# Chunked scan issued in rounds, with two gate units between its steps

## What is computed

```python
h = rms_norm(x, norm1_pre)
q, k, v, z, xbc, dt_raw, gates = split_cols(h @ w_in, IN_SPLITS)
attn_out = gqa_attention(q, k, v) @ w_attn_proj
# ssd_branch: xbc through a width-5 convolution and silu gives xs, bm, cm;
# for each direction (forward, flipped), 16 heads in 2 groups, 4 chunks of 128 tokens:
y_diag = einsum("bclgn,bcsgn->bcgls", cc, bc) * decay_in, times xd
states = einsum(bc, decay_states, xd)
def step(h, inp): st, dec = inp; return h * dec + st, h      # over the chunks
y_off  = einsum(cc, prev, exp(a_cs))
y = y_fwd + y_bwd + d_skip * xs
ssd_out = rms_norm(y * silu(z), ssd_norm) @ w_ssd_proj
g_attn, g_ssd = split(sigmoid(gates))
mixed = (g_attn * attn_out + g_ssd * ssd_out) @ w_out
```

## Time and profile before

| what | value |
|---|---|
| median of 3 runs | 2350.87 us (2345.10 to 2355.63) |
| the profiled execution | 2345.79 us, span 2344.0 us |
| PE busy | 2198.4 us, 94% of the span |
| DVE, ACT, POOL busy | 49%, 43%, 41% |
| mean granted TensorE clock | 0.961 |

### The profile page before, as it was taken

The page is one execution under the profiler, slowest core; times in us unless marked ns, Lnnn a source line. Parts: engine busy times, 40 slices in busy tenths (PEclk is TensorE's granted clock), DMA queues, the critical chain, the costliest instruction groups (busy, mean ns, idle before and its releaser), DMA issues.

```text
span 2344.0 us, 28202 instructions
## 1 busy us (share of the span) xinstructions
PE 2198.4 (94%) x10837; PEld 1826.0 (78%) x10848; DVE 1142.7 (49%) x1836; ACT 1004.5 (43%) x2027; POOL 962.0 (41%) x730
## 2 busy tenths in 40 slices
PE   7999899999988997899999998998899999999997
PEld 5788778888877776778888877785697887888886
DVE  3445565554344666465554363664445335544322
ACT  5666444443235555244443254655243234323222
POOL 3655553433457652444333442224323334322232
PEclk9999999999999999799999997998899999999998
DMA  4111122232213221122222221110012232222221
GB/s 157 55 55 60 49 99 99 90 108 99 94 60 102 82 68 39 62 82 90 98 100 97 88 88 36 37 36 19 19 46 101 88 108 72 92 106 90 101 99 52
DMA packets 29846, 183.08 MB, mean 78 GB/s; under 512 B 3984, under 2 KB 4112, under 8 KB 11920
## 3 DMA queue, kind: packets, MB, share of 16 engines
q1 hardware_dynamic: 29712, 181.27, 22.4%
HBM read 174.97 MB, written 2.10 MB: 76 GB/s over the span
## 4 chain that ended last, share of the span: by engine, by line
PE 82%; DVE 6%; ACT 5%; issue 3%; POOL 2%; DMA 1%; SPq 0%; POOLq 0%; ACTq 0%; DVEq 0%
PE PS L1452 81%; PE PS L1577 1%; POOL LO L2735 1%; DVE bQS L2191 1%; PE PS L1690 0%; ACT HI L1779 0%; DMA RAW<-wall 0%; DVE aQS L2191 0%; DVE T_f L2263 0%; DVE XL L2268 0%; DVE YH L2293 0%; PE PS L1625 0%; POOL cQ L2818 0%; ACT bP L1995 0%; POOL cROT L2810 0%
## 5 line engine op out<-in xcount | busy, mean ns | idle before, releaser
L2735 POOL TENSOR_TENSOR LO<-RAW,HI 128x512 fp32r<-128x512 f32 (+2 forms) x382 | 540.9, 1432 | 601.6 <-ACT HI L1779 601.3
L1452 PE MATMUL PS<-XH,HI 128*128 128x512 f32 (+1 forms) x1584 | 637.6, 403 | 24.5 <-DVE XL L2191 6.7
L1452 PE MATMUL PS<-XH,LO 128*128 128x512 f32 (+1 forms) x1584 | 624.4, 394 | 0.0
L1452 PE MATMUL PS<-XL,HI 128*128 128x512 f32 (+1 forms) x1584 | 618.1, 395 | 1.0 <-DVE XL L2268 1.0
L1779 ACT ACTIVATE HI<-RAW 128x512 fp32r<-128x512 f32 (+3 forms) x668 | 365.4, 608 | 171.3 <-PE PS L1452 168.0
L2191 DVE TENSOR_TENSOR LO<-RAW,HI 128x512 fp32r<-128x512 f32 (+2 forms) x286 | 305.0, 1071 | 246.2 <-ACT HI L1779 245.8
L1452 PEld LDWEIGHTS PS<-XH,HI 128*128 128x128 f32 (+1 forms) x1584 | 302.2, 191 | 87.7 <-issue 20.4
L1452 PEld LDWEIGHTS PS<-XH,LO 128*128 128x128 f32 (+1 forms) x1584 | 301.4, 190 | 65.7 <-issue 0.8
L1452 PEld LDWEIGHTS PS<-XL,HI 128*128 128x128 f32 (+1 forms) x1584 | 300.8, 190 | 62.7 <-DVE XL L2268 2.5
L1452 PE MATMUL PS<-HH,HI 128*128 128x512 f32 x528 | 205.4, 389 | 0.0
L1452 PE MATMUL PS<-HL,HI 128*128 128x512 f32 x528 | 205.4, 389 | 0.0
(11 more groups left out here) (395 smaller groups left out, 3358.3 us busy)
## 6 DMA issues: line engine op xcount, KB each, us to landing
RAW<-wall SPq DMA_DIRECT2D x138, 1024.0 KB, 4.8
RAW<-wall SPq DMA_DIRECT2D x24, 896.0 KB, 4.4
bROT<-bTQ SPq DMA_DIRECT2D x64, 64.0 KB, 2.0
RAW<-wall SPq DMA_DIRECT2D x5, 512.0 KB, 3.3
XF<-xT SPq DMA_DIRECT2D x4, 512.0 KB, 5.2
outT<-XR SPq DMA_DIRECT2D x8, 256.0 KB, 2.0
FP<-cfp SPq DMA_DIRECT2D x1, 1024.0 KB, 6.7
MKF<-cmask SPq DMA_DIRECT2D x1, 704.0 KB, 10.8
```

The costliest lines, as they stand in the source:

```text
L1452: return e.matmul(out, a, b, start=start, stop=stop)
L2735: return e.tensor_tensor(out, x, h.bitcast(F32), ALU.subtract)
```

## The change

The scan is one generator, `scan()`, that goes in rounds. The elementwise part of each step is a step of its own (`se` for the exponentials, `sz`, `sq`, `sv` for DVE's part of `sy`, `so`, `sp`; `sd` for the decay of the state) and stands one round or more behind the matmuls it reads. All heads use banks 2 and 3, `sp` has banks 4 and 5, `so` bank 6, `sy` bank 7. The states are in an order written out by hand (`STATES`), and a state of chunk 1 has a buffer of its own. Gate units `cga` 0 and `cgs` 0 are moved from behind the z units to the scan, which runs beside them at 1.8 pieces a tick. What is left behind the z units begins with `cpa` 0, then `cga` 1, the transposes, and `cps` 0 at once behind these. The sigmoids of both moved gates are taken right after `yn`.

```diff
-    out += [...] + [("cx", j // 2) for j in CONV[::2]] + [("cz", i) for i in range(4)]
-    for i in range(4):
-        out += [("cga", i), ("cpa", i), ("cgs", i), ("cps", i)]
+    out += [...] + [("cx", j // 2) for j in CONV[::2]] + [("cga", 0), ("cgs", 0)]
+    out += [("cz", i) for i in range(4)] + [("cpa", 0), ("cga", 1), ("cps", 0)]
+    for i in range(1, 4):
+        out += [("cga", i)] * (i > 1) + [("cpa", i), ("cgs", i), ("cps", i)]
...
+            r = 0
+            while sdone[0] < 16 or not finished[0]:
+                while item(r - 3) and ("cxt", CONV[-1]) not in steps:
+                    yield
+                if item(r):
+                    put("sw", *item(r))
+                    if item(r)[1]:
+                        put("sd", *item(r))
+                if r < 16:
+                    for dr in range(2):
+                        at_bank(("sh", r, dr), 2 + dr)
+                    put("sh", r)
+                    yield
+                if item(r - 2):
+                    s = put("sv", *item(r - 2))
+                    freed[ag.bank_of[("sp",) + item(r - 2)]] = ("sprv" if s[2] else "sprv0", s)
+                if item(r - 4):
+                    dr, idx, g = item(r - 4)
+                    freed[6] = ("sod", put("sq", dr, idx + 1, g))
+                    finished[0] = r - 4 == len(STATES) - 1
+                if item(r - 1):
+                    s = ("sp",) + item(r - 1)
+                    at_bank(s, 4 + s[1])
+                    put(*s)
+                    yield
+                if r < 16:
+                    s = put("se", r)
+                    for dr in range(2):
+                        freed[2 + dr] = ("sem", s)
+                if item(r - 3):
+                    dr, idx, g = item(r - 3)
+                    at_bank(put("so", dr, idx + 1, g), 6)
+                    yield
+                if 0 < r < 17:
+                    put("em", r - 1)
+                if 2 < r < 19:
+                    freed[7] = ("syd", put("sz", r - 3))
+                    sdone[0] = r - 2
+                if 1 < r < 18:
+                    at_bank(put("sy", r - 2), 7)
+                    yield
...
-        alongside(scans(), RATES[3])
-        until(lambda: sdone[0] >= 4 and all(finished))
+        alongside(scan(), RATES[3])
+        gate("cga", 0, True)
+        gate("cgs", 0, True)
+        until(lambda: sdone[0] >= 4 and finished[0])
+        beside[1] = RATES[7]
...
-        mix_a(0)
+        for kind in ("mga", "mgs"):
+            for j in range(2):
+                put(kind, 0, j)
+        shares(0)
+        gate("cga", 1)
         for j in range(8):
             b, s = pick(), ("yt", j)
...
-        for i in range(4):
-            if i:
-                mix_a(i)
-            mix_b(i)
+        mix(0)
...
-            elif kind == "sh":
+            elif kind == "se":
                 h, = a
                 if h == 0:
                     e.wait_ge(*when("cdec", "cae"))
                 if h > 1:
                     e.wait_ge(*when("sy", "sy", h - 2))
```

More of the change, by code:

```diff
@@ L347, in unit_sequence @@
     out += [("up1", j) for j in range(FF)] + down("dn1")
-    out += [("cq", 0), ("ck", 0), ("cq", 1), ("cv", 0)] + [("cx", j // 2) for j in CONV[::2]] + [("cz", i) for i in range(4)]
-    for i in range(4):
-        out += [("cga", i), ("cpa", i), ("cgs", i), ("cps", i)]
+    out += [("cq", 0), ("ck", 0), ("cq", 1), ("cv", 0)] + [("cx", j // 2) for j in CONV[::2]] + [("cga", 0), ("cgs", 0)]
+    out += [("cz", i) for i in range(4)] + [("cpa", 0), ("cga", 1), ("cps", 0)]
+    for i in range(1, 4):
+        out += [("cga", i)] * (i > 1) + [("cpa", i), ("cgs", i), ("cps", i)]
     out += [("co", i) for i in range(4)]
@@ L1055, in c_times_b @@
             freed[6] = ("scbd", s)
[L1057 to L1091, removed]
-                    yield
[L1093 to L1110, removed]
-                    for dr in range(2):
[L1112 to L1129, removed]
-                    yield
-            for _ in range(2):
-                for dr in range(2):
-                    next(left[dr])
-                    yield
@@ L1136, in scans, with scan, item, skip_term @@
[L1136 to L1142, removed]
+        def scan():
+            skipped = [0]
+            def item(n):
+                return STATES[n] if 0 <= n < len(STATES) and STATES[n] else None
+            def skip_term(n):
+                for h in range(skipped[0], min(16, skipped[0] + n)):
+                    put("y0", h)
+                    skipped[0] = h + 1
+            r = 0
+            while sdone[0] < 16 or not finished[0]:
+                while item(r - 3) and ("cxt", CONV[-1]) not in steps:
+                    yield
+                if item(r):
[3 more added lines that the diff above has]
+                if r < 16:
+                    for dr in range(2):
+                        at_bank(("sh", r, dr), 2 + dr)
+                    put("sh", r)
+                    yield
+                if item(r - 2):
[9 more added lines that the diff above has]
+                    put(*s)
+                    yield
+                if r < 16:
[14 more added lines that the diff above has]
+                    yield
+                if ("cxt", 7) in steps:
+                    skip_term(4)
+                elif skipped[0] < 10:
+                    skip_term(2)
+                r += 1
@@ L1151, in second, with gate, product @@
             c_times_b(g)
[L1152 to L1157, removed]
-        alongside(scans(), RATES[3])
-        until(lambda: sdone[0] >= 4 and all(finished))
+        def gate(kind, i, later=False):
+            for j, t in enumerate(lin_fm((kind, i), "X", evac=lambda j, t: product(kind, i, j, t))):
+                if not later:
+                    put("m" + kind[1:], i, j)
+        def product(kind, i, j, t):
+            freed[tiles[t].bank] = ("mgr", put("mgp", "m" + kind[1:], i, j, t))
+        alongside(scan(), RATES[3])
[3 more added lines that the diff above has]
+        beside[1] = RATES[7]
         for i in range(4):
@@ L1168, in second, with shares, mix @@
         put("yn")
[L1170 to L1172 removed]
+        def shares(i):
             for j, t in enumerate(lin_fm(("cpa", i), "cO")):
                 freed[tiles[t].bank] = ("mpa", put("mpa", i, j, t))
[L1176 to L1178 removed]
+        def mix(i):
             for j, t in enumerate(lin_fm(("cps", i), "cY")):
@@ L1189, in second @@
             ready["cY", j] = ("yl", s)
-        for i in range(4):
-            if i:
-                mix_a(i)
-            mix_b(i)
+        mix(0)
+        for i in range(1, 4):
+            if i > 1:
+                gate("cga", i)
+            shares(i)
+            gate("cgs", i)
+            mix(i)
         for i in range(4):
@@ L2139, in scalar @@
                 act(dst, src, ACT.Copy, scale=col("dskip", h)).then_inc(SEM["sy0"], 1)
-            elif kind == "sp" and a[1] == 0:
+            elif kind == "sv" and a[1] == 0:
                 dr, idx, g = a
-                e.wait_ge(*when("sst", *step))
-                act(blk(PRV, 2 * dr + g), PS[bank][:, :], ACT.Copy).then_inc(SEM["sprv0"], 1)
-            elif kind == "sh":
+                e.wait_ge(*when("sst", "sp", *a))
+                act(state(*a), PS[ag.bank_of[("sp",) + a]][:, :], ACT.Copy).then_inc(SEM["sprv0"], 1)
+            elif kind == "se":
                 h, = a
@@ L2170, in scalar @@
             elif kind in ("mga", "mgs"):
[L2171 to L2174, removed]
+                i, j = a
+                g = gated(kind, i, j)
+                e.wait_ge(*when("mgr", *whole["mgp", kind, i, j]))
+                act(g, g, ACT.Sigmoid).then_inc(SEM[kind], 1)
             elif kind == "mps":
@@ L2672, in vector @@
                 ysum = None
[L2673 to L2678, removed]
+            elif kind == "sv" and a[1]:
+                p = state(*a)
+                e.wait_ge(*when("sst", "sp", *a))
+                e.wait_ge(*when("sxw", "sd", *a))
+                e.tensor_tensor(p, p, PS[ag.bank_of[("sp",) + a]][:, :], ALU.add).then_inc(SEM["sprv"], 1)
             elif kind == "cze":
@@ L2727, in vector @@
                 e.wait_ge(*when("yh", *step))
+                if j == 0:
+                    e.wait_ge(*when("mpa", *whole["mpa", 0, 1]))
                 diff(blk(YTL, j), blk(TT, j % 2), blk(YTH, j)).then_inc(SEM["yl"], 1)
@@ L2828, in gpsimd @@
                 r = 32 * c + 16 * dr + 8 * g
-                if idx or g:
-                    e.wait_ge(*when("sst", "sp", dr, idx - (1 - g), 1 - g))
+                n = STATES.index(a)
+                before = [t for t in STATES[:n] if t and t[0] == dr]
+                if before:
+                    e.wait_ge(*when("sst", "sp", *before[-1]))
                 else:
```

112 lines of the change are left out of this document (71 added, 41 removed).

## The result

| | median | ratio to the kernel before | 95% interval |
|---|---|---|---|
| before | 2349.38 us (4 runs) | | |
| changed | 2404.98 us (4 runs, 2400.32 to 2408.92) | 1.0234 | 1.020 to 1.0267 |

The changed kernel is 2.3% slower, 55.6 us by the medians. The profiled execution took 2408.92 us, with this span on its page and a mean granted clock of 0.946. One of the four executions of the fifth experiment took 7649 us against 2375 to 2379 us for the others; it is left out of that experiment's time.

The account below looks back on a forecast made before the run. It took the scan's rounds to be bound by a serial wait of TensorE on ACT's exponentials, 2.65 us each. Sum: 2345.8 + 20.0 at full clock + 16.6 for the clock = 2382 us, range 2352 to 2404.

Parts of the forecast that it names:

- The serial chain: Scan rounds: sums r-2, exponentials r, exponents r+1 run one after another, 2.65 us a round, 29.2 us in 11 gaps.
- the last sums: End of the scan: the last two sums with their wait for POOL take 5.6 us.
- The work of that stage: Scan from head 4 to the z tiles: TensorE work of 66.6 + 4.4 = 71 us at full clock.
- The clock: Scan from head 4: granted clock stays at 0.81, so 71 us of work become 87.6, 16.6 us more.
- The rival at 0.65: Scan: the clock is down more, to 0.65, giving 38 us and a total of 2404 us; chance 0.13.
- The sum of this stage: Scan from head 4 to the z tiles: work, gaps, last sums with POOL's wait and slow clock, 118.0 us.
- Behind the z tiles: `cpa` 0 to `cps` 0: 7.1 us idle before `cga` 1, then uncovered transpose evacuation, 2.06 us a piece.
- The start of the scan: Scan up to the exponents of head 4: 19.7 us of TensorE work plus four stalls, 28 us.
- The gate units: Moved from behind the z tiles into the scan: 32 blocks of 0.68 us, 21.8 us, costed as moved work.
- Not serial: Scan: ACT meets the sums earlier, the gaps vanish and the clock holds; 2334 us, faster; chance 0.10.
- the tail is hidden: Behind the z tiles: the waits come out covered and the clock holds; 2348 us, no change; chance 0.10.
- the clock holds: Scan: no loss to a lower clock, everything else as forecast; 2366 us; chance 0.20.

Follow-up runs that it names:

- fifth experiment: Against the changed kernel: 12 useless matmuls added behind the sums of heads 0 to 12, one behind heads 13 to 15; 2375.67 us, ratio 1.0109.
- experiment 1: Against the changed kernel: in each scan round the sums of head r-2 stand ahead of the exponents of head r; 2346.26 us, ratio 0.9979.
- second experiment: Against the changed kernel: behind the z tiles `cga` 1 comes ahead of `cpa` 0, and `cgs` 1 ahead of `cps` 0; 2391.23 us, ratio 1.0165.
- rounds alone: Against the changed kernel: same scan in rounds, but both gate units stay behind the z tiles in the old order of units; 2408.72 us, ratio 1.0236.

## Why the prediction was wrong in size

The direction, the mechanisms and their places were right; the measured 2405 us lie 23 above the forecast of 2382 and 1 above the range's upper end, 2404. Step by step:

- **The serial chain.** Right. Forecast 2.65 us from the sums' end to the next exponents. Measured 4.16 - 1.71 = 2.45, and shown to be the cause from two sides: by another order and by another part of EM. Idle time from head 4 to the z tiles was forecast at 30.4 us (29.2, and 1.2 in the last sums, which is 5.6 less 4.4) and is 25.0. The chain is 0.2 us shorter in eleven rounds, 2.2 us; and in four of them a gate block hides 0.75 us, 3.0 us, which the prediction had seen and not taken off.
- **The work of that stage.** 71 us forecast, 76.7 by experiment 1 at a clock of 1.00. Of the 5.7 us, 2.7 are four gate blocks that the sum forgot: it had 9 up to head 4 and 19 behind, 28 of the 32; there were 23 behind. (It also priced the 9 at 6.8 us, where 9 x 0.68 is 6.1.) Another 1.3 us are the sums, which take 1.83 us with exponents behind them, not 1.71, eleven times. The rest was not traced.
- **The clock. This is the step that failed:** "I take the 0.81 that the scan has now: 66.6 + 4.4 = 71 us of work become 87.6, 16.6 us more." It measured 28.5 us (105.3 us busy for 76.7 us of work), so the factor is 0.73. The 0.81 belonged to a scan that had single long waits, 13.8 us idle in 71.5; the new one is idle 1.5 to 2.3 us in every round, and each round behind head 4 has its fall to 1.2 GHz. The row that showed it was in hand: the clock read 1.00 ahead of one idle of 2.41 us and 0.50 behind it. The forecast should have counted how often that happens, not carried over the mean. The rival at 0.65, with a chance of 0.13, gave 2404 us, nearly what was measured, but by luck: its clock term of 38 us is 9.5 too high, which makes up for terms elsewhere that were too low.
- **The sum of this stage.** 130.3 us against 118.0: +5.7 for the work, -5.4 for the idle, +11.9 for the clock (12.2, with rounding 12.3). That the first two cancel is luck.
- **Behind the z tiles.** Right: `cga` 1 began 12.46 us behind the last z matmul (12.5 forecast) after an idle of 6.83 (7.1), the transposes at +25.3 (25.1), `cps` 0 ended at +51.0 (49.6). The second experiment gets 13.4 us of it back.
- **The rest.** The start of the scan took 29.4 us against 28, the z tiles 46.9 against 46.1. With the 12.3 and the 1.4 above, the four stages are 15.9 us over the forecast's 36.6, 52.5 in all, 3.1 short of the 55.6 of the medians. Also, the forecast summed from 2345.8 us, 3.6 below the median of the kernel before. The profiled execution shows 63.1 us, since its scan also begins 8.2 us later than before. That is no effect of the change: the first exponents start anywhere from 1600 to 1609 us in the kernels profiled here, and at 1607.94 in the kernel before with a third part of EM, where they start at 1599.86 in the kernel before. The cause is open.
- **The gate units.** Costed as moved work. That holds where the rounds have no gap: with them (2334 us with both orders right) and without (2331 us) the times are alike within the intervals. In rounds with the gap they were worth some 15 to 19 us.
- **"Not serial", "the tail is hidden", "the clock holds".** None came. As to the first one's price: without the chain the kernel takes 2346 us, where the rival had 2334.

The Trainium skill, "TensorE: Matmul & The Clock Gate", section "A second HAM failure mode: psum-queue depth-cycling", has short idles between groups of matmuls make the clock swing and cost throughput between the bursts. The fifth experiment agrees, with its number: 21.9 us come back in eleven rounds when the idle is filled with work that nobody reads.

## What to carry to other kernels

When a loop is turned into rounds, write the steps of two engines side by side and look for a step of one round that the next engine needs, but that is issued at the round's end: here a buffer's release (the sums) stood last, and the first step of the next round hung on it. Either issue the releasing step first, or add one part to the buffer; one of them is enough, and where the release is early already the part buys nothing. When such a wait is costed, count the idle and the slow clock behind it as two terms (here they came out alike), and take the clock from what follows a single idle of that length, not from the mean of a stage with another pattern.

## What was not expected of the hardware

The idle and the clock are worth about the same: 22.5 us and 21.9 us in eleven rounds. And less work was no faster: rounds alone have no gate blocks between head 4 and head 15, and take 112.85 us where the changed kernel takes 112.62 with them, since the clock is 0.62 and not 0.79. The 23 blocks are 15.6 us of work, but without them the busy time is only 3.0 us less (86.2 against 89.2): 12.6 us of theirs are lost to the lower clock, and 3.3 us to idle that they had covered (26.7 against 23.4).
